# A hybrid Fourier, state-space and attention trunk: one activation table and a Newton step in the head norms, a second PSUM bank for the Fourier halves, and earlier modulation rows

## The reference

```python
mod_l = (silu_c @ w_mod[i] + b_mod[i])[:, None, :]        # six rows of 1024 per layer, for c and for c_ctx
ul = modulate(rms_norm(hl, norm_mix_g[i]), sh1_l, sc1_l)
f = jnp.fft.fft2(ug, axes=(1, 3), norm="ortho")            # even layer, 8 groups of 64 channels, real part kept
qw = rms_norm(qw.reshape(b, l, WIN_Q_HEADS, HEAD_DIM), q_norm_win)   # odd layer, also kw, qn, kn
# rms_norm(x, g) = x * rsqrt(mean(x*x) + 1e-6) * g, over the 64 elements of a head
```

## Time and profile before

| | |
|---|---|
| runs | 1275.67 us median of 3 (1275.34 to 1278.98) |
| the profiled execution | 1275.35 us, of which the trace's span is 1273.6 us |
| PE busy | 1208.5 us, 95% |
| DVE busy | 807.6 us, 63% |
| ACT busy | 600.2 us, 47% |
| POOL busy | 86.5 us, 7% |
| mean granted PE clock | 0.989 |

### The profile page before, as it was taken

One profiled execution on the slowest core, in us unless ns is written; L12 is line 12 of the kernel. 1 busy time (PEld: TensorE's weight loads), 2 busy tenths in 40 slices (PEclk: granted clock), 3 DMA queues, 4 the chain that ended last, 5 costly groups with the idle time before them and its releaser, 6 DMA issues.

```text
span 1273.6 us, 17426 instructions
## 1 busy us (share of the span) xinstructions
PE 1208.5 (95%) x6554; PEld 961.8 (76%) x6554; DVE 807.6 (63%) x1153; ACT 600.2 (47%) x1009; POOL 86.5 (7%) x73
## 2 busy tenths in 40 slices
PE   5799899999998999999999999999989899999998
PEld 3466678787876787687887887885778559888997
DVE  3554488796977564677576675695542795645555
ACT  4531264655647332732331331423978784845543
POOL 0000101002020005000000000044000003000000
PEclk9799999999999999999999999999999999999999
DMA  9457021211121224253453443541233103355554
GB/s 366 199 227 284 38 67 51 67 50 65 53 67 34 66 93 167 104 187 125 173 198 132 173 173 132 198 148 66 83 133 116 34 1 134 125 190 184 185 192 150
DMA packets 41839, 166.38 MB, mean 131 GB/s; under 512 B 4528, under 2 KB 6704, under 8 KB 38704
## 3 DMA queue, kind: packets, MB, share of 16 engines
q1 hardware_dynamic: 41488, 164.97, 36.8%
q10 hardware_dynamic: 288, 0.56, 0.1%
HBM read 164.46 MB, written 1.05 MB: 130 GB/s over the span
## 4 chain that ended last, share of the span: by engine, by line
PE 71%; DVE 14%; ACT 7%; issue 4%; DMA 3%; DVEq 0%; SPq 0%; ACTq 0%
PE ps L1652 47%; PE ps L1659 8%; PE ps L1917 7%; DMA mring<-in_w_mod 2%; DVE cacc L1365 2%; PE ps L1675 1%; DVE sm L1600 1%; ACT ey L1081 1%; ACT u L977 1%; DVE ey L1439 1%; PE ps L1742 1%; DVE prob L1625 1%; ACT w_hi L927 1%; DVE macc L1524 1%; DVE mixF L1465 1%
## 5 line engine op out<-in xcount | busy, mean ns | idle before, releaser
L1216 DVE TENSOR_TENSOR w_lo<-raw,w_hi 128x1024 fp32r<-128x1024 f32 x206 | 258.1, 1253 | 131.3 <-ACT w_hi L927 130.9
L927 ACT ACTIVATE w_hi<-raw 128x1024 fp32r<-128x1024 f32 x206 | 216.6, 1053 | 236.1 <-DMA raw<-in_w_ff 177.9
L1652 PE MATMUL ps<-a_hi,w_hi 128*128 128x512 f32 (+1 forms) x868 | 319.7, 368 | 0.4 <-DVE w_lo L1216 0.4
L1652 PE MATMUL ps<-a_hi,w_lo 128*128 128x512 f32 (+1 forms) x868 | 308.2, 355 | 0.0
L1652 PE MATMUL ps<-a_lo,w_hi 128*128 128x512 f32 (+1 forms) x868 | 308.2, 355 | 0.0
L1652 PEld LDWEIGHTS ps<-a_hi,w_hi 128*128 128x128 f32 x868 | 164.9, 190 | 28.9 <-issue 4.0
L1652 PEld LDWEIGHTS ps<-a_lo,w_hi 128*128 128x128 f32 x868 | 164.9, 190 | 25.3 <-issue 1.2
L1652 PEld LDWEIGHTS ps<-a_hi,w_lo 128*128 128x128 f32 x868 | 164.7, 190 | 23.3
L1652 PE MATMUL ps<-b_hi,w_hi 128*128 128x512 f32 x304 | 119.5, 393 | 0.0
L1652 PE MATMUL ps<-b_lo,w_hi 128*128 128x512 f32 x304 | 118.6, 390 | 0.0
L1652 PE MATMUL ps<-b_hi,w_lo 128*128 128x512 f32 x304 | 118.3, 389 | 0.0
(11 more groups left out here) (253 smaller groups left out, 1701.6 us busy)
## 6 DMA issues: line engine op xcount, KB each, us to landing
raw<-in_w_ff SPq DMA_DIRECT2D x128, 512.0 KB, 3.5
mring<-in_w_mod SPq DMA_DIRECT2D x24, 1024.0 KB, 7.6
mring<-in_w_mod SPq DMA_DIRECT2D x32, 768.0 KB, 5.0
raw<-in_w_in_even SPq DMA_DIRECT2D x36, 512.0 KB, 3.5
raw<-in_w_in_odd SPq DMA_DIRECT2D x18, 512.0 KB, 3.4
raw<-in_w_out_even SPq DMA_DIRECT2D x16, 512.0 KB, 3.5
raw<-in_w_out_odd SPq DMA_DIRECT2D x8, 512.0 KB, 3.5
bias<-in_rpb_na SPq DMA_DIRECT2D x8, 256.0 KB, 3.8
```

The costliest lines, as they stand in the source:

```text
L927: nc.scalar.activation(w_hi[:, u % RING, :, :], raw[:, u % RING, :, :], ACT.Copy).then_inc(hi_done, 1)
L1216: v.tensor_tensor(w_lo[:, u % RING, :, :], raw[:, u % RING, :, :], w_hi[:, u % RING, :, :].bitcast(F32), ALU.subtract).then_inc(lo_done, 1)
L1652: ins = mm(out_ap, w_[:, n % RING, k, :], (x_[k][:, 0:ntok] if type(x_) is list else x_[:, k, 0:ntok]), start=(k == 0 and j == 0), stop=(k ...
```

## The change

Four edits:

1. In `hstat` the logarithm and the exponential come from one table set, loaded once ahead of the first head norm. DVE then refines the result r by one Newton step: x · g · r · (1.5 − 0.5 · v · r²), where v is read from PSUM again. So `hnorm` grows from one DVE instruction to five, and the PSUM bank of the head sums is handed back by DVE's second instruction (`hv_done`) instead of by ACT's logarithm (`var_done`).
2. In `norm` the one-column logarithm is replaced by a plain load of the table.
3. The second Fourier half uses bank 6 (`B_Y`) instead of bank 3.
4. Five of the eight `mod` steps of each pass stand one tile sooner.

```diff
-MOD_AFTER = (0, 2, 4, 6, 8, 9, 11, 12)
+MOD_AFTER = (0, 2, 4, 5, 7, 8, 10, 11)
...
         elif k == "dftw":
             for q in range(2):
-                job(st + (q,), B_AUX[0], freed=("vf_done", 2 * st[1] + q + 1))
+                job(st + (q,), (B_AUX[0], B_Y)[q], freed=("vf_done", 2 * st[1] + q + 1))
...
         elif k == "hstat":
-            n_var += 1
-            job(st, B_AUX[n_aux % 2], freed=("var_done", n_var))
+            job(st, B_AUX[n_aux % 2], freed=("hv_done", nk))
...
-                    nc.scalar.activation(warm[:, 0:1], eps[:, 0:1], ACT.Ln).then_inc(signal(act_seq), 1)
+                    act.preload_act_table_set("natural_log")
...
                 elif k == "hstat":
+                    if qk_n[st[1:]] == 0:
+                        act.preload_act_table_set("natural_log_exp_and_others")
...
-                                         bias=eps[:, 0:1]).then_inc(signal(var_done), 1)
+                                         bias=eps[:, 0:1]).then_inc(signal(act_seq), 1)
...
                     x_ = ktile(*st[1:])
+                    key = ("hstat",) + st[1:]
+                    r_, b = rms_of(key), jobs[key][0]
+                    c_ = u32[:, 0, 0:odd_tokens[st[1:]]]
+                    if qk_n[st[1:]]:
+                        dve.wait_ge(qn_done, qk_n[st[1:]])
+                    v.tensor_tensor(c_, r_, r_, ALU.mult).then_inc(signal(dve_seq), 1)
+                    dve.wait_ge(*latest())
+                    v.scalar_tensor_tensor(out=c_, in0=ps[:, b, 0:odd_tokens[st[1:]]], scalar=HD * EPS, in1=c_, op0=ALU.add, op1=ALU.mult).then_inc(signal(hv_done), 1)
                     v.scalar_tensor_tensor(out=x_, in0=x_, scalar=vt[:, 2, g_q[st[1]]:g_q[st[1]] + 1],
-                                           in1=rms_of(("hstat",) + st[1:]), op0=ALU.mult, op1=ALU.mult).then_inc(signal(qn_done), 1)
+                                           in1=r_, op0=ALU.mult, op1=ALU.mult).then_inc(signal(dve_seq), 1)
+                    dve.wait_ge(hv_done, qk_n[st[1:]] + 1)
+                    v.tensor_scalar(c_, c_, -0.5 / HD, 1.5, ALU.mult, ALU.add).then_inc(signal(dve_seq), 1)
+                    dve.wait_ge(*latest())
+                    v.tensor_tensor(x_, x_, c_, ALU.mult).then_inc(signal(qn_done), 1)
```

More of the change, by code:

```diff
@@ L636, in trunk @@
         mod1_in = [sem(f"mod1_in{i}") for i in range(MR1)]
-        names = ("grow_done htok_done unit_done sines_done mfull_done dtrow_done acc_sq tmp_sq mu_used row_done mcol_done modc_done sil_done hi_done lo_done c0_in dft_in xsq_done xrms_done xr_done xn_done xnt_done xu_done c1_in vec_in wdt_in bias_in dve_seq act_seq consts_set vt_done "
+        names = ("grow_done htok_done unit_done sines_done hv_done mfull_done dtrow_done acc_sq tmp_sq mu_used row_done mcol_done modc_done sil_done hi_done lo_done c0_in dft_in xsq_done xrms_done xr_done xn_done xnt_done xu_done c1_in vec_in wdt_in bias_in dve_seq act_seq consts_set vt_done "
                  "silc_done th0_done h_done sq_done var_done rstd_done nt_done u_done split_done coef_done "
@@ L646, in trunk @@
         S = {n: sem(n) for n in names}
-        (grow_done, htok_done, unit_done, sines_done, mfull_done, dtrow_done, acc_sq, tmp_sq, mu_used, row_done, mcol_done, modc_done, sil_done, hi_done, lo_done, c0_in, dft_in, xsq_done, xrms_done, xr_done, xn_done, xnt_done, xu_done, c1_in, vec_in, wdt_in, bias_in, dve_seq, act_seq,
+        (grow_done, htok_done, unit_done, sines_done, hv_done, mfull_done, dtrow_done, acc_sq, tmp_sq, mu_used, row_done, mcol_done, modc_done, sil_done, hi_done, lo_done, c0_in, dft_in, xsq_done, xrms_done, xr_done, xn_done, xnt_done, xu_done, c1_in, vec_in, wdt_in, bias_in, dve_seq, act_seq,
          consts_set, vt_done, silc_done, th0_done, h_done, sq_done, var_done, rstd_done, nt_done,
```

## The result

The changed kernel takes **1262.49 us** (median of 5 runs, 1261.60 to 1263.89), the kernel before 1275.67; the ratio is 0.9896, 95% interval 0.9881 to 0.9912. That is 13.2 us less, where 11.7 between the medians (11.3 in the sum) was forecast. Two of all the executions, one of the kernel before (2029.96 us, granted clock 0.65) and one of e2_mod (1516.59 us, 0.76), ran far slower than the others at 0.98 to 0.99 and are left out of all times and ratios. The profiled execution took 1263.14 us with a span of 1261.0, so 12.6 us of span went.

The account below looks back on a forecast made before the run. PE was taken as the bound, busy 1208.5 of 1273.6 us. Gains of 4.2 + 3.5 + 3.4 + 0.2 = 11.3 us from the profiled 1275.35 gave 1264.05, rounded to 1264.0 us; range 1261.5 to 1268.0.

Parts of the forecast that it names:

- the three places: Where PE waits: Fourier tiles 4.2 us, end of the last MLP pass 2.06 us, odd layer 3.8 us idle.
- Fourier halves: Fourier tiles: PE's four waits for DVE's copy of the first half go; gain 4.2 us.
- Modulation rows: End of the last MLP pass: PE's wait for the accumulators goes; gain 2.06 + 1.4 (clock) = 3.5 us.
- the wait also cost clock: Behind the wait ahead of the last pass's sum: granted clock 0.53, costing 1.4 us over 3 us.
- spare time of 3.7 us: Last MLP pass: last accumulator pair ends at 861.2, PE asks for the sum at 864.95; spare 3.7 us.
- Head norms: Odd layer: earlier ACT shortens the doubling's first wait; gain 1.9 + 0.3 (rotation) + 1.2 (clock) = 3.4 us.
- rival (b): At the doubling the clock falls anyway (two waits within 3 us): 1265.2 us; chance 0.08.
- DVE's 25.6 us: Odd layer: five-instruction hnorm costs DVE 25.6 us more, 58 of 86.7 us busy, without delaying PE.
- rival (a): Odd layer: VectorE takes ScalarE's place, doubling as late or clock falls again, no gain there: 1267.4 us; chance 0.12.
- Block norms: Ahead of the odd layer and the second MLP: dropping the one-column logarithm gains 0.2 us.
- Rival (c): Last MLP pass: POOL holds up the last `macc` pair, twice 4.3 us, so PE waits: 1266.4 us; chance 0.06.
- Rival (d): Odd layer: new DVE instructions cost far more than priced, so DVE bounds it; 1290 us at three times; chance 0.03.

Follow-up runs that it names:

- e2_mod: The kernel before with only the five modulation steps of a pass one tile sooner: 1273.05 us, ratio 0.9983.
- e11_mod_one_back: The changed kernel with the last modulation step of a pass behind tile 12 again: 1261.77 us, ratio 0.9896.
- e1_bank: The kernel before with only the second Fourier half in bank 6: 1268.54 us, ratio 0.9952.
- e4_preload: The kernel before with only the plain table load in the block norms: 1274.71 us, ratio 0.9997.
- e6: The changed kernel with the head norms' logarithm and exponential from two sets again (26 table loads), Newton step kept: 1269.88 us, ratio 0.9955.
- e5_table_only: The changed kernel without the Newton step, hnorm one DVE instruction again, ACT's logarithm handing the bank back: 1263.16 us, ratio 0.9902.
- e7_two_steps: The changed kernel with a second Newton step in each head norm: 1274.03 us, ratio 0.999.
- e8_dup_before: The kernel before with only the two halves of the key doubling in banks 4 and 5: 1269.32 us, ratio 0.9946.
- e3_heads: The kernel before with only the head norms' single table and Newton step: 1269.02 us, ratio 0.9949.

## Why the prediction held, and where it was off

The time, the range and the three places held. By its own steps:

- **Fourier halves, 4.2 us.** The mechanism was right and the term mis-sized: it measured 5.1 us. I had taken the bracketed waits. From start to start the four tiles lost 1.05, 1.39, 1.39 and 1.32 us, where the rows show 0.78 (the first) and 1.13 (the others): some 0.27 more each in the first three. Two trains of four matmuls stand in the rows as 1.03 and 1.13 us, 2.16 together, yet a train of eight as 1.89. That is the same 0.27: trains that follow each other overlap, and a wait between them takes the overlap away. In the last tile it shows as 0.19, as the `dfts` wait, forecast at about 0.75, grew from 0.78 to 0.86.
- **Modulation rows, 3.5 us.** The wait of 2.06 went and 2.1 us with it. The 1.4 us of clock was in this pair of traces (1.6), but only one of the five traces with the wait shows it. The step that failed is "the wait also cost clock", taken as a fixed price from a single profile. That it was in the very trace that the forecast starts from is luck: without it the three places give 11.1 us in place of 12.7. The spare time of 3.7 us for the last accumulators came out as worked out (3.7). The last step's place is a cure but not the only one (e11_mod_one_back). One sum on the way is off without effect: 1.2 + 1.1 + 3.5 is 5.8, not 5.9.
- **Head norms, 3.4 us.** Up to the head sum of `qn.2` it is 54.01 - 50.05 = 4.0 us, from 903.89 to 957.90 before and from 896.34 to 946.39 after. That is 1.84 of wait, 0.28 at the rotation and 0.24 of broken trains ahead of the doubling (46.70 against 44.33 from the first head sum, 2.4 in all), and 1.6 of clock behind it. The two waits left were forecast at 0.8 and 0.8 and are 0.89 and 0.78. The clock was kept, which rival (b) denied. Behind the long wait (2.72 or 2.73) it fell in each of the five traces that have it (before, e1, e2, e4, e6).
- **DVE's 25.6 us.** By the groups above, the four added instructions take 1.55 us for 256 tokens and 2.48 for 512, 8 x 1.55 + 5 x 2.48 = 24.8. The estimate of 0.3 us for the one-input instruction was 0.285. In the window DVE is at 52.9 and not 58, for two reasons: the last norm stands behind the window, and instructions that follow each other overlap (22.8 us of busy time against e5_table_only). That the work is free is shown by e5_table_only, against rival (a).
- **Block norms, 0.2 us.** e4_preload shows 0.1 us for the one norm inside B. The other lies in D, whose spread hides it.
- **Rival (c), the port.** The last pair took 4.31 us beside POOL, not 8.6. It fell.
- **Rival (d) had its threshold wrong.** I said that DVE must reach 62 us, 2.4 times my price, to eat the gain. At two times (e7_two_steps, 851.1 - 804.0 = 47.1 us of busy time) the gain was already gone: C is 8.4 us over that of the kernel before, which is nearly what A and B gained (5.1 and 3.8). The step that failed compared sums over 87 us; the room is set by the backlog between a norm and the next key copy.
- **Not foreseen:** +1.5 us in the input stage and -1.3 us behind the attention. They nearly cancel, and neither was in the sum.

That the doubling could be freed by a bank, without touching a norm, was not among the rivals. It should have been: the wait was for a bank, and a wait for a bank has two cures.

## What to carry to other kernels

When PE waits for another engine to empty a PSUM bank, first ask for a bank that is idle in that phase: here it gave 5.6 us (e8_dup_before) where the faster engine gave 3.9 (e3_heads), at no cost to DVE. An engine's room is not its idle share of a stage, but what it can fall behind ahead of the next thing that is waited for; in e11_mod_one_back two heavy steps with a light one between cost no wait, where the same two in a row, as late, did. Measure places by start-to-start times in the trace, where a broken train shows, and take clock losses from several traces, not one.

## What the runs showed of the hardware

- A wait costs PE more than its bracket: 0.27 us in each of the first three Fourier tiles beside 0.78 or 1.13, 0.07 us ahead of the sum (270.41 against 268.28 us from sum to sum, for 2.06).
- The granted clock's dips are not tied to one wait. The dip at the scan near 150 us came in e3_heads and e8_dup_before only, two of fourteen traces, with the waits of 1.05, 0.30 and 0.59 us on PE there that the kernel before has too, without a dip. Why it comes in these two isn't shown. In e3_heads, in a window:

```profile
150.00:156.00 6.00, 4.61 (x24) 4.22 (x25) 4.80 (x11) 0.83 (x3) 3.24 (x4) 0.72 0.00 0
```

- The dip at the scan cost 1.7 us (B 758.91 against 757.2), and one at the attention's start only 0.2 (C 141.70 against 141.46), where PE also waits for ACT and DVE. The Trainium skill, page "TensorE: Matmul & The Clock Gate", section "What's actually happening", says that the gate's timing doesn't start anew with a kernel, so that the point of a change moves between executions. The traces agree: the sum and the code around it are the same in the kernel before and in e1_bank, and so is the wait of 2.06 us, yet the execution of before shows a dip there and that of e1_bank none.
- A switch to the combined table set costs the same 1283 ns, and ACT's next instruction starts 0.02 us behind it; its logarithm and exponential take what those of the single sets take (0.47 and 0.42 us for 256 tokens in e8_dup_before and in the changed kernel).
- On DVE an operand in PSUM cost nothing extra: the instruction with one took 424 ns for 256 tokens and 691 for 512 (L1575), the nearest one with all operands in SBUF 475 and 742 (L1576). Beside POOL, DVE slows but isn't held up for whole instructions: a pair of `macc` takes 4.32 us where 3.54 stand alone.
